# Lag kernels of a state-space phase: from a round trip through DRAM to four copies within SBUF, with rows renumbered

## The reference

```
for rev in (0, 1):
    h[t] = abar * h[t-1] + bbar @ u[t]          # complex, 64 states a group
    y[t] += real(cmat @ h[t])                   # 16 channels a group
y = y + d * u
```

## Time and profile before

| what | value |
|---|---|
| median of 3 runs | 1737.36 us (1733.51 to 1750.48) |
| profiled execution | 1738.68 us, span of the trace 1736.9 us |
| PE busy over the span | 1546.6 us (89%) |
| DVE, ACT, POOL busy | 981.4 us (57%), 806.1 us (46%), 661.2 us (38%) |
| state-space phase | from about 556 us to about 918 us of the span |

### The profile page before, as it was taken

One profiled execution on the slowest core, in us unless ns is written; L12 is line 12 of the kernel. 1 busy time (PEld: TensorE's weight loads), 2 busy tenths in 40 slices (PEclk: granted clock), 3 DMA queues, 4 the chain that ended last, 5 costly groups with the idle time before them and its releaser, 6 DMA issues. The chain is left out here.

```text
span 1736.9 us, 28020 instructions
## 1 busy us (share of the span) xinstructions
PE 1546.6 (89%) x11286; PEld 1321.5 (76%) x11286; DVE 981.4 (57%) x1271; ACT 806.1 (46%) x1096; POOL 661.2 (38%) x507
## 2 busy tenths in 40 slices
PE   4799999799698899888658988888999999899998
PEld 0378888588687788778648976677999967689997
DVE  6444522488745277755724646564766655556665
ACT  2422222455413577665454434554554454455452
POOL 0088887599798924563741013311000010110000
PEclk8889999999899999887878999998999999899999
DMA  9966666355535677776657455314544333245541
GB/s 390 425 245 226 225 228 250 131 195 188 216 110 202 158 241 217 240 222 173 188 131 277 161 193 207 146 49 153 207 198 193 145 112 145 89 155 218 200 162 49
DMA packets 118713, 332.72 MB, mean 192 GB/s; under 512 B 30772, under 2 KB 72116, under 8 KB 102344
## 3 DMA queue, kind: packets, MB, share of 16 engines
q1 hardware_dynamic: 115734, 305.63, 49.8%
q10 hardware_dynamic: 2868, 25.54, 4.1%
HBM read 290.55 MB, written 40.58 MB: 191 GB/s over the span
## 5 line engine op out<-in xcount | busy, mean ns | idle before, releaser
L3018 PE MATMUL ffn_ps<-ffn_x_lead,w_lead 128*128 128x256 f32 x672 | 188.5, 280 | 1.1 <-DVE w_rest L3097 1.1
L3018 PE MATMUL ffn_ps<-ffn_x_lead,w_rest 128*128 128x256 f32 x672 | 188.7, 281 | 0.0
L3018 PE MATMUL ffn_ps<-ffn_x_rest,w_lead 128*128 128x256 f32 x672 | 188.5, 281 | 0.0
L401 POOL TENSOR_TENSOR w_rest<-resident_ring,w_lead 128x2048 fp32r<-128x2048 f32 x7 | 32.1, 4579 | 396.5 <-ACT w_lead L397 206.3
L3097 DVE TENSOR_TENSOR w_rest<-resident_ring,w_lead 128x2048 fp32r<-128x2048 f32 x42 | 96.1, 2292 | 83.7 <-ACT w_lead L3062 83.7
L365 PE MATMUL qkvz_ps<-qkvz_w_lead,h_lead 128*128 128x512 f32 x320 | 125.9, 393 | 5.4 <-POOL h_rest L646 5.4
L3018 PEld LDWEIGHTS ffn_ps<-ffn_x_lead,w_lead 128*128 128x128 f32 x672 | 126.2, 188 | 2.2 <-issue 1.5
L3018 PEld LDWEIGHTS ffn_ps<-ffn_x_rest,w_lead 128*128 128x128 f32 x672 | 126.5, 188 | 0.7
L3018 PEld LDWEIGHTS ffn_ps<-ffn_x_lead,w_rest 128*128 128x128 f32 x672 | 126.3, 188 | 0.0
L365 PE MATMUL qkvz_ps<-qkvz_w_lead,h_rest 128*128 128x512 f32 x320 | 125.5, 392 | 0.0
L365 PE MATMUL qkvz_ps<-qkvz_w_rest,h_lead 128*128 128x512 f32 x320 | 125.5, 392 | 0.0
(11 more groups left out here) (518 smaller groups left out, 4526.0 us busy)
## 6 DMA issues: line engine op xcount, KB each, us to landing
resident_ring<-in_ffn_gu SPq DMA_DIRECT2D x22, 2048.0 KB, 9.0
ffn_wd<-in_ffn_down SPq DMA_DIRECT2D x22, 1024.0 KB, 4.8
resident_ring<-in_ada_w SPq DMA_DIRECT2D x8, 2048.0 KB, 13.8
xc<-s_q_scratch SPq DMA_DIRECT2D x128, 128.0 KB
resident_x<-in_s_bT SPq DMA_DIRECT2D x64, 256.0 KB
resident_ring<-in_attn_w_in ACTq DMA_DIRECT2D x8, 2048.0 KB, 10.5
s_W_scratch<-resident_x SPq DMA_DIRECT2D x64, 256.0 KB, 3.3
resident_ring<-in_s_w SPq DMA_DIRECT2D x32, 512.0 KB, 8.3
```

The source lines that it names most:

```text
L401: self.core.nc.gpsimd.tensor_tensor(self.slots[1][0], self._raw(r), self.slots[0][0].bitcast(F32), ALU.subtract).then_inc(self.rest_made, 1)
L3018: last = nc.tensor.matmul(ps[s][f][:, m, :], w_part[w][m][:, k, f * P:(f + 1) * P], x_part[x][:, k, :], start=(k, w, x) == (0, 0, 0), stop ...
```

## The change

The scratch `lags` in DRAM is gone. After ACT's copy, SP issues four DMAs, one for each group of a quad, that read the tile `lags` in SBUF through overlapping windows and write T directly. The partition of `lags` is the outermost dimension of that read, and rows are now numbered channel first (row = channel * 8 + token); the scratch of u, the loads of `ub` and the repeated loads of `InputWeights` follow. T has two buffers, so a load waits for `outputs(k-2)` only. The T copies come right after the store of u in SP's step, ahead of everything else, and the load of `ub` comes right behind the state weights. `b_fw`, `b_bw` and ACT's copies are gone: PE multiplies with partitions 64 to 127 or 0 to 63 of `b_all` and V, all backward products first, then lag 0, then (behind a wait for the backward ones) the forward products.

```diff
@@ InputWeights.load: q and b, repeated rows
-                         ... ap=[[2 * P, CH], [0, SG], [1, 2 * P]])).then_inc(self.q_in[s], 16)
+                         ... ap=[[0, SG], [2 * P, CH], [1, 2 * P]])).then_inc(self.q_in[s], 16)
-                                        ap=[[0, CH], [SN * 2 * P, SG], [1, WB * 2 * P]])).then_inc(self.b_in[s], 16)
+                                        ap=[[SN * 2 * P, SG], [0, CH], [1, WB * 2 * P]])).then_inc(self.b_in[s], 16)
@@ s5_mixer: tiles
-        b_all, b_fw, b_bw = [ph.sb(n, [P, 2, 2, CPAD]) for n in ("b_all", "b_fw", "b_bw")]
+        b_all = ph.sb("b_all", [P, 2, 2, CPAD])
-        T = core.x[:, 0, :].rearrange("p (j m q) -> p j m q", j=4, q=2)
+        T_odd = ph.sb("T_odd", [P, DM])
+        T_raw = [m.rearrange("p (j m) -> p j m", j=4) for m in (core.x[:, 0, :], T_odd[:])]
+        T = [m.rearrange("p j (m q) -> p j m q", q=2) for m in T_raw]
-        def windows(k):
-            return bass.AP(tensor=lagged.tensor, offset=lagged.offset + k * 2 * SG * CG * LAGW, ap=[[2 * SG, CH], [2 * LAGW, SG * 4], [1, 2 * P]])
+        def shifted(j):
+            return bass.AP(tensor=lags_at.tensor, offset=lags_at.offset + 32 * j * 2 * LAGW, ap=[[2 * LAGW, SG], [2 * SG, CH], [1, 2 * P]])
@@ SP, step n
                     if is_ct(n - 1):
                         sp.wait_ge(u_kept, n)
-                        sp.dma_start(bass.AP(tensor=to.tensor, offset=to.offset, ap=[[CH * NCH, CG], [CG * CH * NCH, SG], [1, CH * NCH]]), us[(n - 1) % 2][:]).then_inc(u_stored[(n - 1) % 2], 16)
+                        sp.dma_start(d["u"][n - 1], us[(n - 1) % 2][:].rearrange("p t n -> p (t n)")).then_inc(u_stored[(n - 1) % 2], 16)
+                    if kl == 0:
+                        sp.wait_ge(spilled, 16)
+                        sp.wait_ge(mod.turned, KT)
+                    if is_ct(kl):
+                        sp.wait_ge(l_kept, kl + 1)
+                        if kl >= 2:
+                            sp.wait_ge(y_done, kl - 1)
+                        for j in range(4):
+                            sp.dma_start(T_raw[kl % 2][:, j], shifted(j)).then_inc(T_landed[kl % 2], 16)
+                    if n >= 3 and is_ct(n - 1):
+                        sp.wait_ge(s_done, 2 * (n - 2))
+                        s5_weights_load(core, sp, n - 1)
+                    if is_ct(n - 1):
+                        sp.wait_ge(u_stored[(n - 1) % 2], 16 * ((n - 1) // 2 + 1))
+                        if n >= 4:
+                            sp.wait_ge(s_done, 2 * (n - 3))
+                            sp.wait_ge(ul_made, n - 3)
+                        src = d["u"][n - 1]
+                        sp.dma_start(ub[(n - 1) % 3][:], bass.AP(tensor=src.tensor, offset=src.offset,
+                                                                 ap=[[NCH, P], [SG * CH * NCH, CG], [1, NCH]])).then_inc(ub_landed[(n - 1) % 3], 16)
+                    for u in units(n):
+                        if u + 4 < SsmUnits.UNITS:
+                            sp.wait_ge(rest_made, u + 1)
+                            s5_unit_load(core, sp, u + 4)
...
-                    if is_ct(kl):
-                        sp.wait_ge(l_kept, kl + 1)
-                        of = lagged[kl]
-                        sp.dma_start(bass.AP(tensor=of.tensor, offset=of.offset, ap=[[LAGW * 2, 4], [4 * LAGW * 2, 2 * SG], [1, LAGW * 2]]),
-                                     lags[:].rearrange("m w q -> m (w q)")).then_inc(lag_stored, 16)
...
-                        sp.dma_start(ub[(n - 1) % 3][:], bass.AP(tensor=src.tensor, offset=src.offset,
-                                                                 ap=[[NCH, CH], [CH * NCH, SG * CG], [1, NCH]])).then_inc(ub_landed[(n - 1) % 3], 16)
...
-                    if is_ct(kl):
-                        sp.wait_ge(lag_stored, 16 * (kl + 1))
-                        sp.wait_ge(y_done, kl)
-                        sp.dma_start(core.x[:, 0, :].rearrange("p (j m) -> p j m", j=4), windows(kl)).then_inc(T_landed, 16)
@@ POOL
-                for b in (b_all, b_fw, b_bw):
-                    g.memset(b[:], 0.0).then_inc(cleared, 1)
+                g.memset(b_all[:], 0.0).then_inc(cleared, 1)
@@ PE, lag_kernels
-                    pe.wait_ge(b_copied, k + 1)
+                    pe.wait_ge(b_landed[s], 16 * (k // 2 + 1))
...
-                                nc.tensor.matmul(out(j, slice(0, P - SG)), b_bw[:, s, c, at(j)], V[:, r % RING, c, j, SG:P], start=c == 0, stop=c == 1)
+                                last = nc.tensor.matmul(out(j, q, slice(0, P - SG)), b_all[hi, s, c, at(j, q)], V[hi, (2 * k + q) % RING, c, j, SG:P], start=c == 0, stop=c == 1)
+                    last.then_inc(behind_done, 1)
...
+                    pe.wait_ge(behind_done, k + 1)
...
-                                last = nc.tensor.matmul(out(j, slice(P, LAGW)), b_fw[:, s, c, at(j)], V[:, r % RING, c, j, 0:P - SG], start=c == 0, stop=c == 1)
+                                last = nc.tensor.matmul(out(j, q, slice(P, LAGW)), b_all[lo, s, c, at(j, q)], V[lo, (2 * k + q) % RING, c, j, 0:P - SG], start=c == 0, stop=c == 1)
@@ PE, outputs
-                    pe.wait_ge(T_landed, 16 * (k + 1))
+                    pe.wait_ge(T_landed[k % 2], 64 * (k // 2 + 1))
@@ ACT
-                def direct(k):
-                    act.wait_ge(b_landed[k % 2], 16 * (k // 2 + 1))
-                    sc.activation(b_fw[lo, k % 2, :, 0:P], b_all[lo, k % 2, :, 0:P], ACT.Copy)
-                    sc.activation(b_bw[hi, k % 2, :, 0:P], b_all[hi, k % 2, :, 0:P], ACT.Copy).then_inc(b_copied, 1)
...
-                            act.wait_ge(lag_stored, 16 * kl)
+                            act.wait_ge(T_landed[(kl - 1) % 2], 64 * ((kl - 1) // 2 + 1))
```

More of the change, by code:

```diff
@@ L1569, in s5_mixer @@
         y_done, y_kept, turned, g_made, cleared, feed_made = [sem(n) for n in "y_done y_kept turned g_made cleared feed_made".split()]
-        lag_stored, T_landed, g_stored, z_stored, feed_in = [sem(n) for n in "lag_stored T_landed g_stored z_stored feed_in".split()]
+        g_stored, z_stored, feed_in = [sem(n) for n in "g_stored z_stored feed_in".split()]
+        T_landed = [sem(f"T_landed{s}") for s in range(2)]
         ub_landed = [sem(f"ub_landed{s}") for s in range(3)]
@@ L1583, in s5_mixer @@
         is_ct = lambda k: 0 <= k < CT
-        lagged = d["lags"]
-        def windows(k):
-            return bass.AP(tensor=lagged.tensor, offset=lagged.offset + k * 2 * SG * CG * LAGW, ap=[[2 * SG, CH], [2 * LAGW, SG * 4], [1, 2 * P]])
+        lags_at = lags[:].rearrange("m w q -> m (w q)")
+        def shifted(j):
+            return bass.AP(tensor=lags_at.tensor, offset=lags_at.offset + 32 * j * 2 * LAGW, ap=[[2 * LAGW, SG], [2 * SG, CH], [1, 2 * P]])
         with ph.block() as block:
@@ L1627, in later_loads @@
                     if n == 3:
-                        sp.wait_ge(cleared, 3)
+                        sp.wait_ge(cleared, 1)
                         for k in range(2):
@@ L1770, in lag_kernels @@
                         pe.wait_ge(feed_made, 1)
+                    out = lambda j, q, cols: ps_l[32 * j:32 * j + 32, q, cols]
+                    at = lambda j, q: slice((4 * q + j) * SG, (4 * q + j) * SG + 32)
                     for q in range(2):
-                        r = 2 * k + q
-                        out = lambda j, cols: ps_l[32 * j:32 * j + 32, q, cols]
-                        at = lambda j: slice((4 * q + j) * SG, (4 * q + j) * SG + 32)
                         for c in range(2):
                             for j in range(4):
-                                nc.tensor.matmul(out(j, slice(0, P - SG)), b_bw[:, s, c, at(j)], V[:, r % RING, c, j, SG:P], start=c == 0, stop=c == 1)
+                                last = nc.tensor.matmul(out(j, q, slice(0, P - SG)), b_all[hi, s, c, at(j, q)], V[hi, (2 * k + q) % RING, c, j, SG:P], start=c == 0, stop=c == 1)
+                    last.then_inc(behind_done, 1)
+                    for q in range(2):
                         for c in range(2):
@@ L1780, in lag_kernels @@
                                 cols = slice((4 * q + j) * SG, (4 * q + j + 1) * SG)
-                                nc.tensor.matmul(out(j, slice(P - SG, P)), b_all[:, s, c, at(j)], cn[:, s, cols] if c else cc[:, k % 4, 0, cols], start=c == 0, stop=False)
+                                nc.tensor.matmul(out(j, q, slice(P - SG, P)), b_all[:, s, c, at(j, q)], cn[:, s, cols] if c else cc[:, k % 4, 0, cols], start=c == 0, stop=False)
                         for j in range(4):
-                            nc.tensor.matmul(out(j, slice(P - SG, P)), core.ident[:, 32 * j:32 * j + 32], feed[:, r, :], start=False, stop=True)
+                            nc.tensor.matmul(out(j, q, slice(P - SG, P)), core.ident[:, 32 * j:32 * j + 32], feed[:, 2 * k + q, :], start=False, stop=True)
+                    pe.wait_ge(behind_done, k + 1)
+                    for q in range(2):
                         for c in range(2):
```

(6 more changed lines are left out.)

32 lines of the change are left out of this document (3 added, 29 removed).

## The result

The changed kernel takes 1726.03 us in the median of six runs (1720.52 to 1728.99), the kernel before 1739.8 (1733.51 to 1750.48): ratio 0.991, 95% interval 0.988 to 0.993. Run again beside the first experiments it was 0.992 (0.990 to 0.995). The forecast was 1706; 14 us by the medians, 16 by the ratio, of the 32 came.

The account below looks back on a forecast made before the run. In the state-space phase PE was near the bound only in the first stretch; T came last in seven steps (38.5 us). 15.5 + 12 - 4.2 - 1.8 = 21.5, plus 10.4: 31.9 off 1738.7 is 1706.8, forecast 1706 us, range 1693 to 1731.

Parts of the forecast that it names:

- Step (1): Output products' waits for T(1), T(3), T(6), T(7), up to step 17, all go: gain 15.5 us.
- (2): Half clock of PE behind T's waits, in state matmuls, output products and lag kernels, goes: gain 12 us.
- (3): V comes next: new waits for V at lag_kernels(3) and (5), cost 4.2 us.
- Step (4): Two more changes of PE's tiling in each lag_kernels, 0.2 us a tile: cost 1.8 us.
- Step (5): ACT's copies into b_fw and b_bw and two POOL memsets go: taken as 0.
- Step (6): SP's units, z, g and small loads now behind T's issues; all used one to three steps later: 0.
- Step (7): From step 18 to lag_kernels(15), scan, outputs and V form the chain without T: gain 0.
- Step (8): Last T takes 7 us from copy to products instead of 17.4: gain 10.4 us.
- B: V takes T's place in full, 2 us more on each V: 12 us lost, 1718 us; chance 0.20.
- C: Copies queue behind weights, SP delays ub and units, only the end gains: 1728 us; chance 0.12.
- D: The four T copies become the bound, slower: 1776 us if T takes 12 us; chance 0.10.
- E: More gain: clock term at 21.1, last T 12.8, switches nil, 45.2 us in all: 1693 us; chance 0.08.

Follow-up runs that it names:

- e5: Changed kernel plus six useless PE matmuls ahead of lag_kernels(3) and of lag_kernels(5), filling the waits for V; ratio 0.990 to the kernel before.
- e1: Changed kernel with z stored ahead of the four T copies of its step; ratio 0.989 to the kernel before.
- e7: Changed kernel with each T copy issued a second time, to a DRAM scratch, and the output products waiting for all eight; ratio 1.006 to the kernel before.
- e8: Changed kernel with lags through DRAM, T's two buffers and four loads kept, the store in its old shape (4 outermost); ratio 0.993 to the kernel before.
- e6: Changed kernel with lags through DRAM again: one store of contiguous rows, four loads at the old place, two T buffers kept; ratio 0.987 to the kernel before.
- e14: Kernel before with only the load of T split into four DMAs, the store's shape kept; ratio 0.996 to the kernel before.
- e9: Kernel before with a second T buffer, room made through ub and z's buffer; ratio 1.001 to the kernel before.
- e13: Kernel before with lags stored as 128 rows in line and T loaded by four DMAs, a second run; ratio 0.987 to the kernel before.
- e12: Kernel before with lags stored as 128 rows in line, T loaded by four DMAs, V in seven quad buffers; 1710.7 us, ratio 0.983.
- e0: Changed kernel run again, unedited, as base of the experiments; ratio 0.992 to the kernel before.

## Why the forecast was half right

- **Step (1), right.** All waits for T up to step 17 are gone.
- **Steps (2) and (3), the first failure.** V's new waits were sized well: 2.35 and 1.01, 3.4 us for a forecast of 4.2. What failed is that I gave back the whole half clock of T's waits (12 us) and put no half clock behind V's, though they take their place. Each burst in the two profiles against its length at full clock: behind T's waits 12.9 us before the change, behind V's waits 7.1 us after it, where the sum has nothing; behind the turn of the outputs, which is in both, 1.6 us more than before. So 15.5 + 12.9 - 3.4 - 7.1 - 1.8 - 1.6 = 14.5, for the 14.8 us measured. e5 shows by experiment that it is the clock: it gets 4.8 to 5.8 us back without moving V.
- **Step (4), right.** The lag kernels of a tile take 2.33 us at full clock where they took 2.11, 0.22 for 0.2. No run tells the tiling from the rest of the new lag kernels.
- **Step (5), right.** ACT busy fell by 13 us over the span, and its lateness, where there is any, is z's.
- **Step (6), the second failure.** "All are used one to three steps later, so 0" was argued from the consumers of loads. z's store has another one: ACT can't overwrite `zb` until it has landed, and that stands ahead of the lead copies, DVE's part and PE's gate projection. e1 gets 5.9 us back, 5.4 of them in the middle stretch, which then takes 94.7 us (before the change 93.7), and e7 shows the loss grow with what stands in front; the last 1.0 us stays open. The step did name the price of a failed cover, a projection a few us late, and set it at nothing.
- **Step (7)** fell with (6): V(15)'s chain starts with `outputs(12)`, which comes only 7.3 us earlier than before (864.21 against 871.55), though `lag_kernels(9)` came 14.9 us earlier. With z first (e1) B is 9.4 us shorter than before, for the 10.4 of steps (7) and (8).
- **Step (8), right**: 7 us from copy to products forecast, 7.65 measured. (Its lower bound is a slip: 17.4 less 2.4 and 8.9 is 6.1, not 6.7.)
- **The rivals.** B named V, but priced it by POOL's speed, not by the clock. C came nearest to the second failure, since it had SP pass a delay on, but to `ub` and the units, not to z's store; its 1728 lies near the measured 1726 by luck, because it keeps T's waits before step 18, and those went. D is refuted (e7, A). E held the fact that matters. The 16 DMA engines of the core and a DMA's outermost dimension were in it as a sentence beside the sum; e8 against e6 shows what it is worth in this kernel: outermost 4, 8.4 us, outermost 128, 2.05. The Trainium skill, DMA: Bandwidth & Descriptors, section Why a DMA increments its semaphore by 16 and not by 1, says that the outermost dimensions set how many of the engines a DMA uses; the two times agree with that, the engines themselves were not counted. I used it as a bonus for the new code and did not ask what the old code would be with a mended store.

So the gain is real, but the way within SBUF is not needed for it. T was late mostly because its store was slow and SP stood behind it (16 us), and in part because it was loaded in one DMA (7 us, e14); the second buffer alone gains nothing in the whole (e9), and the DRAM trip with a quick store is as good (e6, e13). How the changed kernel's own gain divides among copies, buffer, place and order is not shown: e8 keeps the slow store and is as fast. The store of u and the load of `ub` have new shapes in the change too; no run takes them alone, but e12 and e13 keep the old ones and lose nothing by it that shows.

## What to carry to other kernels

Before a round trip is removed, time its two halves: if one DMA lands several times later than others of its size, look at its outermost dimension first, for that is a one-line change. When a wait goes, find the next one and price it with the half clock behind it, or fill it with work. And when a queue is reordered, follow the stores too: the engine that waits to reuse a buffer is a consumer.

## What the runs showed of the hardware

- 2.35 us idle of PE came before 9 us at half clock (1.2 GHz), from 685.67 to about 694.6, in the changed kernel, and 1.01 us before V(5)'s lag kernels came before half clock until about 725 (the projection took 7.99 us). In e5 useless matmuls and then 1.27 us idle came before none. So it isn't the length of the idle time alone.
- The clock can also fall elsewhere at one run and not at the next. In the second model's first layer, 10 us of the same code, granted clock 0.66 in the changed kernel's profile and 1.00 in e0's:

```profile
1102.40:1112.40 10.00, 7.10 (x24) 6.00 (x25) 2.40 (x4) 3.82 (x7) 0.00 (x0) 0.66 0.54 210
```

```profile
1103.90:1113.90 10.00, 7.51 (x40) 5.95 (x40) 2.00 (x4) 4.46 (x8) 0.00 (x0) 1.00 0.54 210
```

  From its first matmul into `even_ps` to its last the layer takes 104.3 us in the one and 99.3 in the other, as much as several of the steps that were weighed here.
- A 128 KB copy within SBUF from 16 partitions landed 4.1 us after its issue in the median, four together, with their issues and up to the products, 7.65; the same windows read from DRAM (e6) 5.5 to 5.7 in the median. A 240 KB store to DRAM took 2.05 us with 128 outermost (e6) and 8.4 with 4 (e8), to the issue of the loads that wait for it.
